# Two weight blocks' products of one token tile at the sub-layer boundary, in the place of products that nobody reads

## The reference

```
h = modulate(rmsnorm(x, g_pre), shift, scale)
a, b = jnp.split(h @ w_in, 2, axis=-1)
h = (jax.nn.silu(a) * b) @ w_out
return x + FFN_RES * gate * rmsnorm(h, g_post)
```

## Time and profile before

| | |
|---|---|
| median of three runs | 3286.37 us (3283.35 to 3288.70) |
| profiled execution, its own time | 3282.8 us |
| its span | 3280.9 us |
| granted PE clock, mean over the span | 0.971 of full |
| PE busy, share of the span | 94% |
| data read from memory | 509 MB, 156 GB/s |

### The profile page before, as it was taken

One profiled execution on the slowest core, in us unless ns is written; L12 is line 12 of the kernel. 1 busy time (PEld: TensorE's weight loads), 2 busy tenths in 40 slices (PEclk: granted clock), 3 DMA queues, 4 the chain that ended last, 5 costly groups with the idle time before them and its releaser, 6 DMA issues. The chain is left out here.

```text
span 3280.9 us, 48857 instructions
## 1 busy us (share of the span) xinstructions
PE 3083.7 (94%) x19610; PEld 2836.7 (86%) x19610; DVE 2155.5 (66%) x2879; ACT 1139.0 (35%) x1941; POOL 575.8 (18%) x578
## 2 busy tenths in 40 slices
PE   6999879999999999999999997679999999979999
PEld 5999758999899998998999997468998999868998
DVE  4777486777776657776876535647777877585444
ACT  3222454223422424223322433234224222454222
POOL 1112101112111111112111102642112112201001
PEclk8999999999999999999999998679999999999999
DMA  7666414666565446665665443024664766313443
GB/s 267 199 206 185 146 43 134 198 217 190 184 196 173 115 123 192 193 211 168 206 205 149 128 127 98 15 68 156 216 201 148 225 203 204 112 43 95 126 127 97
DMA packets 565510, 515.80 MB, mean 157 GB/s; under 512 B 42965, under 2 KB 499238, under 8 KB 563494
## 3 DMA queue, kind: packets, MB, share of 16 engines
q1 hardware_dynamic: 565286, 512.68, 51.0%
HBM read 509.37 MB, written 3.24 MB: 156 GB/s over the span
## 5 line engine op out<-in xcount | busy, mean ns | idle before, releaser
L1342 PE MATMUL bank<-h_hi,w_hi 128*128 128x384 f32 x3328 | 1116.8, 336 | 3.8 <-DVE tmp L1801 3.8
L1344 PE MATMUL bank<-h_hi,w_lo 128*128 128x384 f32 x3328 | 1114.8, 335 | 0.0
L1343 PE MATMUL bank<-h_lo,w_hi 128*128 128x384 f32 x3328 | 1114.2, 335 | 0.0
L1757 DVE TENSOR_TENSOR w_lo<-raw,w_hi 128x1024 fp32r<-128x1024 f32 x648 | 804.1, 1267 | 411.8 <-ACT w_hi L1603 406.9
L1603 ACT ACTIVATE w_hi<-raw 128x1024 fp32r<-128x1024 f32 x648 | 679.1, 1059 | 1015.7 <-PE bank L1375 483.8
L1779 DVE SCALAR_TENSOR_TENSOR fold<-ada_raw,cond,fold 128x1024 f32<-128x1024 f32 x462 | 638.5, 1438 | 0.0
L1342 PEld LDWEIGHTS bank<-h_hi,w_hi 128*128 128x128 f32 x3328 | 625.6, 188 | 12.9 <-DVE tmp L1801 6.0
L1343 PEld LDWEIGHTS bank<-h_lo,w_hi 128*128 128x128 f32 x3328 | 625.5, 188 | 5.8
L1344 PEld LDWEIGHTS bank<-h_hi,w_lo 128*128 128x128 f32 x3328 | 625.3, 188 | 0.0
L2069 POOL TENSOR_TENSOR h_lo<-tmp,h_hi 128x384 fp32r<-128x384 f32 x176 | 284.9, 1619 | 1786.5 <-DVE h_hi L1805 1786.5
L1371 PE MATMUL bank<-w_hi,h_hi 128*128 128x512 f32 x1056 | 334.4, 398 | 0.0
(11 more groups left out here) (200 smaller groups left out, 2512.0 us busy)
## 6 DMA issues: line engine op xcount, KB each, us to landing
raw<-w_ffn_in SPq DMA_DIRECT2D x352, 512.0 KB, 5.0
ada_raw<-w_ada SPq DMA_DIRECT2D x272, 512.0 KB, 4.2
raw<-w_ffn_out SPq DMA_DIRECT2D x176, 512.0 KB, 4.8
raw<-w_hgrn_in SPq DMA_DIRECT2D x40, 512.0 KB, 4.7
g_rows<-g_dram SPq DMA_DIRECT2D x12, 1024.0 KB, 6.8
raw<-w_attn_qkv SPq DMA_DIRECT2D x24, 512.0 KB, 5.3
raw<-w_conv_in SPq DMA_DIRECT2D x24, 512.0 KB, 4.9
ada_first<-w_ada SPq DMA_DIRECT2D x16, 512.0 KB, 10.6
```

Source lines behind the costliest of these rows:

```text
L1342: mm(out, wh, h_hi[:, k, :], start=(k == 0), stop=False)
L1343: mm(out, wh, h_lo[:, k, :], start=False, stop=False)
L1344: last = mm(out, wl, h_hi[:, k, :], start=False, stop=(k == DC - 1))
L1757: V.tensor_tensor(w_lo[:, b % RING, :], raw[:, b % RAW, :], w_hi[:, b % RING, :].bitcast(F32), ALU.subtract).then_inc(w_lo_made, 1)
```

## The change

A new `first_tile(s, banks, half)` does the products of the first two weight blocks with `h_hi` of token tile 0 alone (128 columns), chunks 0 to 3 for half 0 and 4 to 7 for half 1. In each boundary half 0 and half 1 stand between the transposes of tiles 1 and 2, where the unread products stood; in a late boundary `fold_up` comes ahead of half 0 and `ada_turn` between the two. The four unread products after tile 2's transposes go without replacement. `first_blocks` does tiles 1 and 2 alone with `h_hi` (256 columns) in every sub-layer but the first; its products with `h_lo` keep all 384. Ahead of all this PE waits for `hf` of tile 0, both halves, and for `a_read` and `b_read` out of an FFN. Where the next sub-layer is an FFN, the fold's two banks are 0 and 1 in the place of 6 and 7, on ACT and DVE too.

```diff
         def first_blocks(s, banks):
             b0, n = first_block[s], 2 * NT * (s + 1)
+            rest = slice(P, T) if s > 0 else slice(0, T)
...
-                            mm(psum[bank][:, 0:T], w[:, (b0 + j) % RING, k * P:(k + 1) * P], h_hi[:, k, :],
-                               start=(k == 0 and w is w_hi), stop=False)
+                            mm(psum[bank][:, rest], w[:, (b0 + j) % RING, k * P:(k + 1) * P], h_hi[:, k, rest],
+                               start=(s == 0 and k == 0 and w is w_hi), stop=False, skip_group_check=True)
...
+        def first_tile(s, banks, half):
+
+            b0 = first_block[s]
+            pe.wait_ge(h_high_made if half else h_low_made, 2 * NT * s + 2)
+            for j, bank in enumerate(banks):
+                pe.wait_ge(w_lo_made, b0 + j + 1)
+                for k in range(4 * half, 4 * half + 4):
+                    for w in (w_hi, w_lo):
+                        mm(psum[bank][:, 0:P], w[:, (b0 + j) % RING, k * P:(k + 1) * P], h_hi[:, k, 0:P],
+                           start=(k == 0 and w is w_hi), stop=False, skip_group_check=True)
+
+        def first_banks(s):
+
+            return (6, 7) if sub_kind[s] == "ffn" else (0, 1)
...
             if e < N_SUB:
                 turn_normed(e, 1)
-                if late_fold(s) is not None:
-
-                    pe.wait_ge(a_read, FC * ffn_number(e))
-                    pe.wait_ge(b_read, FC * ffn_number(e))
-                    fold_up(late_fold(s), 6)
-                    ada_turn(late_fold(s), 7)
-                    unread_products(8)
-                else:
-                    if sub_kind[s] == "ffn":
-                        pe.wait_ge(a_read, FC * (ffn_number(s) + 1))
-                    unread_products(16)
+                late, first = late_fold(s), first_banks(e)
+                if sub_kind[s] == "ffn":
+                    pe.wait_ge(a_read, FC * (ffn_number(s) + 1))
+                    pe.wait_ge(b_read, FC * (ffn_number(s) + 1))
+                pe.wait_ge(hf_low, NT * e + 1)
+                pe.wait_ge(hf_high, NT * e + 1)
+                if late is not None:
+                    fold_up(late, first[0] ^ 6)
+                first_tile(e, first, 0)
+                if late is not None:
+                    ada_turn(late, first[1] ^ 6)
+                first_tile(e, first, 1)
                 turn_normed(e, 2)
-                unread_products(4)
```

More of the change, by code:

```diff
@@ L1364, in first_blocks @@
                     last = mm(psum[bank][:, 0:T], w_hi[:, (b0 + j) % RING, k * P:(k + 1) * P], h_lo[:, k, :],
-                              start=False, stop=(k == DC - 1))
+                              start=False, stop=(k == DC - 1), skip_group_check=True)
                 last.then_inc(block_done, 1)
+        def first_tile(s, banks, half):
[9 more added lines that the diff above has]
+            return (6, 7) if sub_kind[s] == "ffn" else (0, 1)
         def out_tile(b, t, hi, lo, opens, closes):
@@ L1434, in out_tail @@
                 turn_normed(e, 1)
-                if late_fold(s) is not None:
-                    pe.wait_ge(a_read, FC * ffn_number(e))
-                    pe.wait_ge(b_read, FC * ffn_number(e))
-                    fold_up(late_fold(s), 6)
-                    ada_turn(late_fold(s), 7)
-                    unread_products(8)
-                else:
-                    if sub_kind[s] == "ffn":
-                        pe.wait_ge(a_read, FC * (ffn_number(s) + 1))
-                    unread_products(16)
+                late, first = late_fold(s), first_banks(e)
[10 more added lines that the diff above has]
+                first_tile(e, first, 1)
                 turn_normed(e, 2)
-                unread_products(4)
-                if late_fold(s) is not None:
-                    pe.wait_ge(mods_made, late_fold(s) + 1)
+                if late is not None:
+                    pe.wait_ge(mods_made, late + 1)
         def ada_half(half, bank, slab):
@@ L1702, in boundary @@
                     if late_fold(e - 1) is not None:
-                        ada_copy(2 * late_fold(e - 1), 6)
+                        ada_copy(2 * late_fold(e - 1), 0 if sub_kind[e] == "ffn" else 6)
                     y_squares_after(e, 2)
@@ L1946, in boundary @@
                 if late_fold(e - 1) is not None:
-                    mod_add(late_fold(e - 1), 7)
+                    mod_add(late_fold(e - 1), 1 if sub_kind[e] == "ffn" else 7)
                 hi_of(e, 1, 0)
```

## The result

| | before | changed |
|---|---|---|
| median of 12 runs each | 3286.57 us (3281.15 to 3289.79) | 3296.98 us (3290.47 to 3304.08) |
| ratio | | 1.0033, interval 1.0025 to 1.0042 |
| span of the profiled execution | 3280.9 us | 3293.5 us |
| granted clock, mean | 0.971 | 0.965 |

The change makes the kernel 0.33% slower, 10.4 us, where the sum said 3.9. The time is in the stated range; most of the loss is the first rival's, the clock. The changed kernel's runs also spread over 13.6 us, before's over 8.6.

The account below looks back on a forecast made before the run. PE's products and DVE's `h_lo` were taken to end the boundaries nearly together, hiding PE's saving. Late boundaries +4.3 us and ordinary ones -0.4 gave +3.9, 3290.3 us on the median; range 3284 to 3303.

Parts of the forecast that it names:

- the sum: Whole kernel: late boundaries +4.3 us and ordinary ones -0.4 make +3.9 us, 3290.3 on the median; chance 0.58 as it stands.
- first rival: Boundaries: the clock falls to half during the narrow products; +10.5 us in three ordinary ones, 3311 in all six; chance 0.20.
- What bounds the boundary: Boundary end: PE's products and DVE's `h_lo` end nearly together, so L1364 starts 0.19 us earlier, not 2.1.
- 256-column product: L1358's shrunk products: 0.113 us each instead of 0.175, saving 21.8 us of PE time, leaving 1.9 us idle before L1364.
- the chain behind it: Behind boundaries into an FFN: DVE's `w_lo` and gate product follow L1907; seven PE waits, 3.8 us, so no gain there.
- The narrow product: 128-column tile-0 products in each boundary: taken at 0.112 us each, set by the weight load.
- the rival at 0.224: Boundaries: each narrow product is worked as two records, costing 41 us, 3327 in all; chance 0.09.
- Late boundaries: Five boundaries with the fold: it waits 0.70 us for `hf`; 0.73 us each into two mixers, 0.96 into three FFNs, 4.3 together.
- Ordinary boundaries: Six boundaries without the fold: tile 2's transposes not late; four gain 0, two into mixers 0.19 us each, -0.4 together.
- the page rule weighed in the prediction: Clock at boundaries: lost only after an idle gap longer than any in the forecast, so the clock holds.
- The size of a fall: Ordinary boundary at low clock: 3.2 us over the 32 narrow products, about 3.5 with the next steps.
- Late boundaries are filled better: Late boundaries, within the clock rival: fuller than ordinary ones; falls were priced only for the six ordinary boundaries.

Follow-up runs that it names:

- experiments 8: The change with freed late fold and all gaps filled, plus tile 0's sixteen `h_lo` products split off ahead of the last `h_lo` wait: 3284.7 us, ratio 0.9996.
- 9: The change with freed fold, filled gaps and split `h_lo` products, plus DVE's first gate product moved ahead of the seventh weight block's low part: 3272.44 us, ratio 0.9957.
- 12: The change with freed fold and filled gaps, `h_lo` products unsplit, plus DVE's first gate product moved ahead of the seventh block's low part: 3277.85 us, ratio 0.9978.
- experiment 1: The change with unread products put back into the three gaps it opened (3, 6 and 6): 3287.7 us against 3284.86 before, ratio 1.0009.
- experiment 3: The change with the late fold freed from the wait for `hf` and half the narrow products behind tile 2's transposes there: 3290.8 us, ratio 1.0020.
- 5: The change with freed late fold and unread products filling the gaps of ordinary and late boundaries: 3287.22 us, ratio 1.0005 to the kernel before.
- experiment 2: The kernel before without its unread products at all eleven boundaries, nothing in their place: 3306.63 us, ratio 1.0067.
- experiment 4: The change with freed late fold and ordinary boundaries' gaps filled; late ones filled only ahead of the `h_lo` products: 3290.81 us, ratio 1.0014.
- experiment 11: The change as given, plus DVE's first gate product moved ahead of the seventh weight block's low part: 3292.8 us, ratio 1.0028 to the kernel before.

## Why the prediction was right and where it was wrong

**What bounds the boundary: right.** That DVE's `h_lo` ends beside PE's products, so that the saving of the 256-column products turns into an idle ahead of the `h_lo` products, is what the profile of the change shows (11.6 us of waits) and what experiments 8, 9 and 12 show together: the split puts the idle to use, and with the moved step beside it the time falls. The idle is 1.5 us and not 1.9, for the 256-column product took 0.123 us and not 0.113. That the chain behind it, down to the product with the gate, is next was named too; that it isn't DVE's work but a load in front of it in DVE's order was not seen.

**The narrow product: right.** 0.115 us against 0.112 at full clock; the rival at 0.224 fell.

**Late boundaries: the wait right, its price only in part shown.** 4.3 us were forecast; the stretches of experiment 1's profiled execution have 4.2, its medians 2.8 for everything. The three into an FFN bear the forecast out: 0.96 each was forecast, 6 and 9 stand at 0.9 in the change's profile, and taking the wait away (experiment 3) brings the three back to before's or near it. For the two into an attention mixer the stretches move by more than a microsecond between executions, so their 0.73 each is not shown, and the medians of experiments 1 and 5 don't tell the freed fold from the waiting one.

**Ordinary boundaries: wrong.** "Nothing is late" there held at the full clock only (+0.1, -0.3, +0.4 and -0.2 us at 5, 7, 8 and 11). The step that failed is the choice of the sum as it stands, at 0.58, over the clock at 0.20: falls in some boundaries are the regular case, and cost 7.6 us (change against experiment 1). That the time lies in the range all the same is owed to the range having been drawn out to four falls, and to a fall in an ordinary boundary costing less than it was priced at; the sum's own path doesn't give it. The rows that should have weighed more were in sight: in the kernel before PE at that place does dense unread work and the clock holds, in the HGRN core it falls after a stretch with 4.88 of 6.00 us busy; the new stretches ahead of the falls have 5.44 of 7.30, 4.89 of 6.90 and 4.66 of 6.80. They say that a fall is possible, not where: boundaries 5 and 8 have 5.45 of 7.30 and keep the clock. What picks the boundary stays open. By the page rule weighed in the prediction (the Trainium skill, "TensorE: Matmul & The Clock Gate", "Why this matters for your kernels") no boundary should have fallen: the longest idle in the stretch ahead of boundary 2's fall is 1.18 us. The trace disagrees, and so do the five late boundaries of experiment 2, where it is 2.2 us, less than the 4.3 to 4.4 of its ordinary ones; those have an idle of the kind that the rule names and say nothing against it.

**The size of a fall: wrong in two ways.** "Late boundaries are filled better" is refuted: boundary 3 fell in the profile, boundary 6 in experiment 4. And 3.5 us for a fall in an ordinary boundary was too much for the change as it ran, 1.9 and 1.8 measured; in experiment 3's profile the ordinary ones stand at 1.7, 3.8 and 1.3 (4, 7 and 11; the HGRN core lies in the stretch of 7). The narrow products do cost the 3.2 worked out, `h_hi` ends 3.5 us later (546.65 against 543.17), but DVE's `h_lo` then comes alone:

```profile
546.75 1.29 DVE L1923 TENSOR_TENSOR h_lo<-hf,h_hi 128x512 fp32r<-128x512 f32 x2
...
540.62 4.97 POOL L2055 TENSOR_TENSOR h_lo<-hf,h_hi 128x512 fp32r<-128x512 f32 x4 [2.52 <-DVE h_hi L1903]
```

POOL is done at 545.59, and DVE's pair takes 1.29 us in the place of 3.45; it ends at 548.04, 1.3 us later than before. In the late boundary the fall and the fold's wait together cost 5.0.

**A slip in the range.** Its upper end, 3303, is said to be falls in four boundaries; at the 3.5 us taken for one that is 3290.3+14.0=3304.3. The measured median is below either.

**Where the sum ends.** Falls 7.6 us, and 2.8 for what experiment 1 leaves, most of it the late boundaries by its profile: the two make the 10.4. How often a boundary falls varies between executions (experiment 11's profile has five, the change's three), which fits the wider spread of the change's runs. The mean granted clock of each run points the same way: 0.965 to 0.967 in the four fastest of the twelve, 0.962 in the two slowest (3300.47 and 3304.08 us). At which boundaries the others fell is not recorded.

## What to carry to other kernels

Work that nobody reads can be what holds TensorE's clock: before real work replaces it, look at the granted clock behind the place, over several executions, and put filler back where the replacement leaves gaps. When a saving doesn't arrive, take its covers away in order and watch which wait grows; with two covers, removing either one alone brings next to nothing of it. And a wait put down to an engine that is itself idle points at that engine's order: here moving one product ahead of the step that waited for a weight block's load took 6.9 us off 3286, as much as the reworked change gave on top.

## What was not expected of the hardware

- DVE's subtraction over 128x512 takes 0.65 us alone and 1.73 beside POOL's (pairs of 1.29 and 3.45 us). A delay of 3.5 us ahead of it came out behind as 1.3. The Trainium skill ("SBUF — State Buffer", "SBUF: two separate sides") has the reason: the port pair that the two engines share is held by one of them for a whole instruction, and the other waits. The trace agrees: in the kernel before, at the second boundary, the two engines' subtractions end in turn, POOL's at 544.48 us, DVE's at 545.03, POOL's at 546.18, DVE's at 546.73, DVE's each time 0.55 us behind POOL's.
- The clock fell behind stretches where PE's records look well filled, 5.34 of 7.30 us in experiment 4, and held behind others just as full. A record of a narrow product lasts 0.28 us at a distance of 0.115, so records overlap.
- The unread products are worth 21.8 us, 0.67% of the kernel (experiment 2).
